# Turning attention probabilities on VectorE and by DMA through HBM in place of TensorE transposes

## What is computed

```python
def chunked_rel_attention(q, k, v, rel_bias):      # 8 heads of 64, 512 positions
    ...
    scores = jnp.einsum("bnqhd,bnkhd->bnhqk", qc, kb) * (dh ** -0.5)
    ...
    scores = jnp.where(valid, scores + bias[None, None], NEG_INF)
    p = jax.nn.softmax(scores, axis=-1)
    out = jnp.einsum("bnhqk,bnkhd->bnqhd", p, vb)

def hybrid_layer(x, norm_gain, w_in, w_out, rel_bias, cos, sin):
    ...
    y = jnp.concatenate([ya * jax.nn.silu(ag.astype(jnp.float32)),
                         yr * jax.nn.silu(rg.astype(jnp.float32))], axis=-1).astype(x.dtype)
    return x + y @ w_out.astype(x.dtype)
```

## Time and profile before

| | us |
|---|---|
| median of 3 runs | 1205.54 (1205.5 to 1205.58) |
| the profiled execution | 1205.41 |
| its span, first to last instruction | 1203.6 |
| PE busy in it | 1195.3 |
| DVE busy | 804.2 |
| ACT busy | 552.8 |
| POOL busy | 374.4 |

### The profile page before, as it was taken

One profiled execution on the slowest core, in us unless ns is written; L12 is line 12 of the kernel. 1 busy time (PEld: TensorE's weight loads), 2 busy tenths in 40 slices (PEclk: granted clock), 3 DMA queues, 4 the chain that ended last, 5 costly groups with the idle time before them and its releaser, 6 DMA issues.

```text
span 1203.6 us, 15005 instructions
## 1 busy us (share of the span) xinstructions
PE 1195.3 (99%) x5822; PEld 1007.5 (84%) x5822; DVE 804.2 (67%) x1402; ACT 552.8 (46%) x954; POOL 374.4 (31%) x275
## 2 busy tenths in 40 slices
PE   9999999999999999999999999999999999999998
PEld 7888888888888888888888889898888889898886
DVE  5878735466888536663568776666866866667875
ACT  6567532324444314332434465654334556654433
POOL 0135289997000000000000227765303023465200
PEclk9999999999999999999999999999999999999999
DMA  8233332323323322333223343433223334442251
GB/s 303 75 126 136 108 112 88 105 77 99 105 88 107 103 88 88 105 105 98 78 83 109 116 137 140 137 132 99 79 70 89 120 129 139 135 138 83 88 146 71
DMA packets 47000, 133.42 MB, mean 111 GB/s; under 512 B 4944, under 2 KB 11600, under 8 KB 46928
## 3 DMA queue, kind: packets, MB, share of 16 engines
q1 hardware_dynamic: 46496, 132.01, 33.7%
q10 hardware_dynamic: 432, 0.44, 0.1%
HBM read 114.08 MB, written 2.10 MB: 97 GB/s over the span
## 4 chain that ended last, share of the span: by engine, by line
PE 95%; DVE 2%; DMA 1%; POOL 1%; ACT 1%; issue 0%; ACTq 0%
PE ps L297 93%; PE ps L249 2%; DVE RA L274 1%; POOL FA L290 1%; DMA RA<-FA 0%; PE ps L551 0%; PE ps L492 0%; DVE FA L286 0%; ACT RA L266 0%; DVE FA L813 0%; DMA FA<-pvec 0%; DVE FA L274 0%; ACT FA L271 0%; ACT FA L270 0%; ACT RA L270 0%
## 5 line engine op out<-in xcount | busy, mean ns | idle before, releaser
L297 PE MATMUL ps<-RA 128*128 128x512 f32 (+1 forms) x5470 | 1176.7, 375 | 1.8 <-POOL RA L555 1.3
L297 PEld LDWEIGHTS ps<-RA 128*128 128x128 f32 x5470 | 974.0, 188 | 182.2 <-POOL RA L555 1.3
L274 DVE TENSOR_TENSOR RA<-FA,RA 128x1024 fp32r<-128x1024 f32 (+6 forms) x303 | 322.9, 1077 | 173.2 <-ACT RA L266 171.4
L266 ACT ACTIVATE RA<-FA 128x1024 fp32r<-128x1024 f32 (+5 forms) x338 | 280.7, 855 | 343.6 <-PE ps L297 177.6
L290 POOL TENSOR_SCALAR FA<-FA 128x256 f32<-128x256 f32 (+3 forms) x117 | 143.3, 1237 | 163.9 <-DVE FA L294 162.8
L286 DVE SCALAR_TENSOR_TENSOR FA<-ps,FA 128x512 f32<-128x512 f32 (+4 forms) x161 | 102.1, 638 | 90.7 <-PE ps L297 44.5
L274 POOL TENSOR_TENSOR FA<-FA 128x512 f32<-128x512 f32 (+1 forms) x82 | 108.9, 1330 | 87.0 <-ACT FA L270 66.7
L274 POOL TENSOR_TENSOR RA<-FA,RA 128x512 fp32r<-128x512 f32 (+1 forms) x37 | 69.6, 1890 | 109.6 <-ACT RA L266 109.6
L1233 POOL MEMSET FA<- 64x64 f32 x2 | 0.2, 144 | 328.7 <-ACT RA L266 328.7
L271 ACT ACTIVATE FA<-FA 128x512 f32<-128x512 f32 (+4 forms) x108 | 59.6, 552 | 80.4 <-DVE FA L1419 66.4
L270 ACT ACTIVATE FA<-ps,FA 128x512 f32<-128x512 f32 x56 | 38.1, 684 | 108.3 <-PE ps L297 108.3
(11 more groups left out here) (49 smaller groups left out, 278.4 us busy)
## 6 DMA issues: line engine op xcount, KB each, us to landing
FA<-w_units SPq DMA_DIRECT2D x188, 512.0 KB, 3.5
UA<-FA SPq DMA_DIRECT2D x32, 320.0 KB, 2.5
RA<-FA SPq DMA_DIRECT2D x10, 512.0 KB, 3.2
FA<-w_units SPq DMA_DIRECT2D x8, 384.0 KB, 3.0
FA<-x SPq DMA_DIRECT2D x8, 256.0 KB, 6.0
FA<-x_rows SPq DMA_DIRECT2D x4, 512.0 KB, 9.2
FA<-rel SPq DMA_DIRECT2D x16, 128.0 KB, 3.3
FA<-dmat SPq DMA_DIRECT2D x8, 256.0 KB, 2.8
```

The source lines that it names most:

```text
L266: return lambda eng: eng.activation(dst, src, ACT.Copy)
L274: return lambda eng: eng.tensor_tensor(dst, a, b, op)
L297: return lambda e: e.matmul(dst, a, b, start=start, stop=stop_)
```

## The change

The probabilities of block 2's attention heads are no longer scaled and no longer turned on PE. In `half_soft` a new `half_store` has DVE turn 128x640 as 32x32 squares into a staging buffer (`vt`); SP then stores it in four DMAs (one for each block of 32 partitions, in runs of 640 bytes) to a tensor in HBM, so that the squares land in their turned places. `half_load`, one slot later, loads the 128x640 back into `TPF` in rows of 2560 bytes. `half_split` reads that instead of PSUM, two slots after the scores as before. The values stay three slots after.

The reciprocals of the sums are taken once for a head, turned by DVE (`rt`), stored to HBM as a row (`rs`) and loaded as a broadcast over 64 partitions (`rl`, `spread_rows`); POOL multiplies the gated output by them, in one more instruction for each pair of heads.

Other edits: in `pieces_after`, `m` and `e` are queued ahead of the `pl`; seven weight low parts of each layer go from POOL to DVE (`POOL_LOW` keeps `g5` and `g6`), and so does the low part of the retention heads' q; in layer 0, `z` waits for the `vt` of its slot; the accumulator `ACC` is freed by `yl` and no longer by `yg`.

```diff
-POOL_LOW = {f"{l}{u}" for l in range(2) for u in ("q0", "v7", "k5", "q6", "q7", "k7", "g5", "g6", "g7")}
+POOL_LOW = {f"{l}{u}" for l in range(2) for u in ("g5", "g6")}
...
-                G(f"z.{k}", [f"f1q.{k}", f"0x.f{k}"], ts(hk, hk, F(PV + PV_GF + k, 1), ALU.mult))
+                G(f"z.{k}", [f"f1q.{k}", f"0x.f{k}", f"0vt.{(k + 2) // 2}.{k % 2}"], ts(hk, hk, F(PV + PV_GF + k, 1), ALU.mult))
...
-                (G if w == "q" else V)(f"{key}.l", [f"{key}.h"], sub(R(lo), F(t), Rf(h)))
+                V(f"{key}.l", [f"{key}.h"], sub(R(lo), F(t), Rf(h)))
...
-                    for i in pair:
-                        V(f"{pre}r.{h}.{i}", [f"{pre}e.{h}.{i}"], recip(F(RD2 + i, 1), F(DE + i, 1)))
-                    for i in pair:
-                        w = 128 * (i + 1)
-                        pc = PB + hoff[i]
-                        G(f"{pre}pn.{h}.{i}", [f"{pre}r.{h}.{i}"], ts(F(pc, w), F(pc, w), F(RD2 + i, 1), ALU.mult))
-                    dma(f"{pre}pm.{h}.{half}", [f"{pre}pn.{h}.{i}" for i in pair] + take(f"tp{half}"),
-                        U(TP + 640 * half, 640).bitcast(F32), F(PB + 640 * half, 640), f"pm{half}")
-                    for i in pair:
-                        free(f"pb{i}", f"{pre}pm.{h}.{half}")
+                    half_store(h, half)
...
-            def half_turn(h, half):
-                for n, i in enumerate(((3, 0), (2, 1))[half]):
-                    ...
-                    for j in range(i + 1):
-                        after = [f"{pre}pm.{h}.{half}"] + take(f"bank{b}") if j == 0 else []
-                        T(f"{pre}pT.{h}.{i}" if j == i else None, after,
-                          turn(bank(b, 128, 128 * j), U(TP + hoff[i] + 128 * j, 128)))
+            def half_store(h, half):
+                pair = ((3, 0), (2, 1))[half]
+                V(f"{pre}vt.{h}.{half}", [f"{pre}e.{h}.{i}" for i in pair] + take("vt"), lambda e: e.transpose(
+                    steps(F(VT, 1), [[32, 5], [160, 4], [1, 32]]), F(PB + 640 * half, 640).rearrange(
+                        "p (t c j) -> p t c j", t=5, c=4)))
+                for i in pair:
+                    free(f"pb{i}", f"{pre}vt.{h}.{half}")
+                for a in range(4):
+                    dma(f"{pre}st.{h}.{half}" if a == 3 else f"{pre}st.{h}.{half}.{a}",
+                        [f"{pre}vt.{h}.{half}"] + (take(f"turned{half}") if a == 0 else []),
+                        bass.AP(turned[half].tensor, turned[half].offset + 160 * a, [[640, 32], [20480, 4], [1, 160]]),
+                        steps(F(VT, 1, 32 * a, 32 * a + 32), [[160, 4], [1, 160]]), f"st{half}")
+                free("vt", f"{pre}st.{h}.{half}")
+                if half == 1:
+                    V(f"{pre}r.{h}", [f"{pre}e.{h}.{i}" for i in range(4)] + ["fill.2"], recip(
+                        steps(F(RDC, 1), [[8, 4], [1, 1]]), F(DE, 4).rearrange("p (i o) -> p i o", o=1)))
+                    V(f"{pre}rt.{h}", [f"{pre}r.{h}"] + take("rdt"), lambda e: e.transpose(F(RDT, 32), F(RDC, 32)))
+            def half_load(h, half):
+                dma(f"{pre}ld.{h}.{half}", [f"{pre}st.{h}.{half}"] + take(f"tp{half}"),
+                    TPF[0:128, 640 * half:640 * half + 640], turned[half], f"ld{half}")
+                ...
+                    dma(f"{pre}rs.{h}", [f"{pre}rt.{h}"] + take(f"rows{h % 2}"),
+                        rows[h % 2].rearrange("(n j) -> n j", j=32), FA[0:128:8, RDT:RDT + 32], "rs")
+            def spread_rows(h):
+                ...
+                dma(f"{pre}rl.{h}", [f"{pre}rs.{h}", "gemm.0q0"] + (take("db") if h % 2 == 0 else []), Rf(DB, 512, p, p + 64),
+                    rows[h % 2].rearrange("(o n) -> o n", o=1).to_broadcast([64, 512]), "rl")
...
-                for c in fins + splits + fins + splits + soft:
-                    next(c, 0)
+                for h, half in loads:
+                    half_load(h, half)
+                for c in fins:
+                    next(c, 0)
+                for c in splits:
+                    next(c, 0)
+                for c in fins:
+                    next(c, 0)
+                for c in soft:
+                    next(c, 0)
+                for c in splits:
+                    next(c, 0)
```

More of the change, by code:

```diff
@@ L51 @@
 PR = Z + 26368
+DB = Z + 29952
 R_COLS = Z + 30720
-TP, TI = 0, 1280
+TI = 0
 T_COLS = TI + 128
@@ L230, in two_blocks_kernel @@
         UA = ctx.enter_context(nc.sbuf_tensor("UA", [128, T_COLS], F32R))
+        TPF = ctx.enter_context(nc.sbuf_tensor("TPF", [128, 1280], F32))
+        turned = [nc.dram_tensor(f"turned{i}", (128, 640), F32, kind="Internal").ap() for i in range(2)]
+        rows = [nc.dram_tensor(f"rows{i}", (512,), F32, kind="Internal").ap() for i in range(2)]
         PS = [ctx.enter_context(nc.psum_tensor(f"ps{i}", [128, 512], F32)) for i in range(8)]
@@ L1224, in two_blocks_kernel @@
             return finish()
-        NM, DE, RD2 = columns(4), columns(4), columns(4)
+        NM, DE, RDC, RDT = columns(4), columns(4), VT + 640, VT + 672
         SS2, MS2, RC2, R12, TMP2 = columns(4), columns(4), columns(4), columns(4), columns(4)
@@ L1233, in two_blocks_kernel @@
             G(f"fill.{i}", ["acl.21", "sin"], lambda e, i=i: e.memset(F(HK + 512 * i, 64, 0, 64), MASKED))
+        G("fill.2", ["sin"], lambda e: e.memset(F(RDC, 32), 1.0))
         zero("z2", K2P, 2048, ["gemm.br7"])
@@ new lines, in half_load @@
+            def half_load(h, half):
+                dma(f"{pre}ld.{h}.{half}", [f"{pre}st.{h}.{half}"] + take(f"tp{half}"),
+                    TPF[0:128, 640 * half:640 * half + 640], turned[half], f"ld{half}")
+                free(f"turned{half}", f"{pre}ld.{h}.{half}")
+                if half == 1:
+                    dma(f"{pre}rs.{h}", [f"{pre}rt.{h}"] + take(f"rows{h % 2}"),
+                        rows[h % 2].rearrange("(n j) -> n j", j=32), FA[0:128:8, RDT:RDT + 32], "rs")
+                    free("rdt", f"{pre}rs.{h}")
@@ L1456, in half_split @@
+            def spread_rows(h):
+                p = 64 * (h % 2)
+                dma(f"{pre}rl.{h}", [f"{pre}rs.{h}", "gemm.0q0"] + (take("db") if h % 2 == 0 else []), Rf(DB, 512, p, p + 64),
+                    rows[h % 2].rearrange("(o n) -> o n", o=1).to_broadcast([64, 512]), "rl")
+                free(f"rows{h % 2}", f"{pre}rl.{h}")
             def half_split(h, half):
@@ L1460, in half_split @@
                     if h < 8:
[L1461 to L1464, removed]
+                        tile = (hoff[i] - 640 * half) // 128
+                        src = steps(TPF[0:128, 640 * half + 32 * tile:640 * half + 32 * tile + 1],
+                                    [[32, i + 1], [160, 4], [1, 32]])
+                        d = lambda c, i=i: steps(R(c + 128 * i, 128), [[384, i + 1], [32, 4], [1, 32]])
+                        parts.append((i, src, d(P2H), d(P2L), f"{pre}ld.{h}.{half}", None))
                     else:
@@ L1472, in half_split @@
                     V(f"{pre}pl.{h}.{i}", [f"{pre}ph.{h}.{i}"], sub(dl, src, dh.bitcast(F32)))
-                    free(where, f"{pre}pl.{h}.{i}")
+                    if where:
+                        free(where, f"{pre}pl.{h}.{i}")
+                if h < 8:
+                    free(f"tp{half}", *[f"{pre}pl.{h}.{i}" for i in ((3, 0), (2, 1))[half]])
             def head_values(h):
@@ L1499, in head_finish @@
                         p = h // 2
[L1500 to L1504, removed]
+                        G(f"{pre}ym.{p}", [f"{pre}yr.{h}", f"{pre}yr.{h - 1}", f"{pre}gt.{p}"],
+                          mul(F(ACC), F(ACC), F(SG + 512 * (p % 2))))
+                        free(f"sg{p % 2}", f"{pre}ym.{p}")
+                        G(f"{pre}yg.{p}", [f"{pre}ym.{p}", f"{pre}rl.{h}", f"{pre}rl.{h - 1}"], mul(
+                            F(ACC).rearrange("p (i a j) -> p i a j", i=4, a=4), F(ACC).rearrange("p (i a j) -> p i a j", i=4, a=4),
+                            steps(Rf(DB, 1), [[32, 4], [128, 4], [1, 32]])))
+                        free("db", f"{pre}yg.{p}")
                         def split():
-                            A(f"{pre}yh.{p}", [f"{pre}yg.{p}"], copy(R(YAH + 512 * p), F(t)))
-                            G(f"{pre}yl.{p}", [f"{pre}yh.{p}"], sub(R(YAL + 512 * p), F(t), Rf(YAH + 512 * p)))
-                            free(tn, f"{pre}yl.{p}")
+                            A(f"{pre}yh.{p}", [f"{pre}yg.{p}"], copy(R(YAH + 512 * p), F(ACC)))
+                            G(f"{pre}yl.{p}", [f"{pre}yh.{p}"], sub(R(YAL + 512 * p), F(ACC), Rf(YAH + 512 * p)))
+                            free("acc", f"{pre}yl.{p}")
                         later.append(split)
@@ L1561, in pieces_after @@
                 turns = lag(2, False) + lag(1, True)
+                loads = lag(1, False)
                 news = scores_at.get(s, [])
@@ L1564, in pieces_after @@
                     head_values(h)
-                for h, half in turns:
-                    half_turn(h, half)
+                    if h < 8:
+                        spread_rows(h)
```

8 lines of the change are left out of this document (2 added, 6 removed).

## The result

| | before | after |
|---|---|---|
| median, us | 1205.56 (1205.5 to 1205.6) | 1192.88 (1192.41 to 1194.84) |
| ratio, with its 95% interval | | 0.9898 [0.9881, 0.9915] |
| the profiled execution, us | 1205.41 | 1192.73 |
| its span, us | 1203.6 | 1190.9 |

The kernel is 12.7 us faster. On another chip, beside the last three experiments, it took 1193.06 us (1192.99 to 1194.43) against 1205.77, a ratio of 0.9898 [0.9884, 0.9913]. The lines of the program have moved: 302 is now every matmul, 279 a two-input operation, 271 an ACT copy, 295 a scaling, 208 a DMA from SP, 1445 the `vt`, 1425 the maxima; where an experiment adds a line, the numbers behind it are one higher.

The account below looks back on a forecast made before the run. PE (TensorE), busy 1195.3 of 1203.6 us, was taken to bound the kernel. 1205.5 - 12.8 (transposes removed) + 1.0 (waits from POOL contention in layer 0) = 1193.7 us, range 1191.8 to 1203.0.

Parts of the forecast that it names:

- The way the kernel is bound: Whole run: PE is busy 1195.3 of 1203.6 us, so each microsecond of PE work removed is worth a microsecond.
- 32 groups, 12.8 us: Block 2: 32 groups of five PE transposes, alternating 0.38 and 0.42 us, go; 12.8 us is the whole possible gain.
- `vt`, 0.85 us: VectorE's 32x32 transpose of 128x640 per half was estimated at 0.85 us, between 0.61 and 1.23.
- Price on the path: nothing: Slot 9: `vt` falls into time where VectorE sat idle or did reciprocals that go, so it costs PE nothing.
- Stores and load: Way through HBM: stores land in 2.3 to 3.2 us, load issued at once, 2 to 3 us room before the high part.
- Order on VectorE: Maxima ahead of `pl`: room before the values of 1.9 to 0.9 us in slot 9, 1.1 to 0.2 in slot 11.
- z and x1 in layer 0, 1.0 us: POOL's z and x1, now later, delay wl; PE waits at values of heads 0 to 3, 0 to 2.0 us, taken 1.0.
- The moved low parts, 0, bounds 0 to +1 a layer: 14 weight low parts and retention heads' q low parts go from POOL to VectorE: 0, bounds 0 and +1 us a layer.
- The sum: Whole kernel: 1205.5 - 12.8 + 1.0 = 1193.7 us.
- Rival 1: PE waits for `pl` at most heads, 0.3 to 0.6 us for each of 16: 1197.5 to 1202.3 us; chance 0.17.
- Rival 2: Staging buffer sets the beat: `vt` waits for stores, binding from a 3.9 us landing; 1215 us at 4.6; chance 0.13.
- rival 3: No change: either of the other two rivals stops near break-even, 1203 to 1208 us; chance 0.06.

Follow-up runs that it names:

- the last three experiments: Each against the changed kernel: `vt` done twice, 1201.69 us; `z` not waiting for `vt`, 1195.01 us; load issued ahead of the row of sums, 1193.22 us.
- The removal alone: The kernel before without its 160 PE transposes and nothing in their place, so probabilities stay unturned: 1193.19 us, ratio 0.9896.

## Why the prediction was right, step by step

- **The way the kernel is bound.** Right: PE stayed at 99%, and the time fell by what left PE. The forecast of 1193.7 lies 0.8 us above the median. But two terms missed, and they cancel in part.
- **32 groups, 12.8 us.** Too small. I lined up the matmuls of the two traces one by one, leaving out the 160: across the attention of the two layers the changed kernel gains 6.8 and 7.3 us, 14.1 in all, 0.44 us a group. The earlier trace rows show only 0.38 and 0.42 for the five transposes; a whole beat there, 0.38 + 7.35 + 0.42 + 6.21, is 14.36 us, and the same two slots now take 13.47 (from the values at 765.14 to those at 778.61), 0.89 less. So the matmuls between also got 0.09 us shorter, why is not shown: the whole beat was the number to take, not the transposes in it. The removal alone gains 14.5 by the same count, and loses 1.7 again where PE enters the retention heads.
- **`vt`, 0.85 us.** Right: 0.844. By the figure of the page "VectorE: DVE Perf Modes" of the Trainium skill (The three transpose paths) I had estimated 1.6; the measurement decides. Its advice (Rules for kernel authors) to leave such a transpose to TensorE didn't hold here, where TensorE bounds the kernel.
- **"Price on the path: nothing".** Right for one, and with less to spare than I wrote: a second one costs 8.6 us.
- **Stores and load.** Stores landed in 2.1 us, below my 2.3 to 3.2. The load took 4.1, above 3.2: here I was wrong. It is issued right behind a weight unit, or a unit and a row; in the kernel where it goes out behind its stores it took 2.9, while the stores, now behind the weight unit, took 3.5. "Issued at once" was wrong too: for every second half SP came to the load only 1.0 us (the median) after the stores had landed. In the slot that I laid out, counted from the end of `vt`, the stores had landed after 3.2 us (forecast 4.2 to 4.8), the load went out at 5.0 and landed at 10.4 (forecast 6.9 to 8.0). So the 2 to 3 us of room before the high part weren't there: its start lay under 0.1 us behind the landing in 14 of 32 halves and over 2 us in only two. ScalarE's 11 waits are the result. What took them up is the room behind the high part, which I had named without a number.
- **Order on VectorE.** I gave rooms of 1.9 to 0.9 and 1.1 to 0.2 us. They came out at 0.07 to 1.57 in layer 0 and 0.90 to 2.02 in layer 1, 0.18 at the place of the earlier trace rows. Right on the whole, with two of 16 below my smallest. What I didn't see is that the order is needed: the old one costs 18.5 us, first of all at the maxima.
- **z and x1 in layer 0, 1.0 us.** Wrong in place: PE waited at no values of heads 0 to 3. The room of head 4, 0.18, went to another POOL instruction beside wl, the multiplication by the sums, which I had put down at nothing; at head 5, with 0.07, no POOL instruction ran, and wl had waited for ScalarE's high part.
- **The moved low parts, 0, bounds 0 to +1 a layer.** Inside the bounds: PE is 0.5 us late once in each layer, at the first retention head's low parts.

```profile
831.95 1.29 POOL L279 TENSOR_TENSOR FA<-FA 128x512 f32<-128x512 f32 x1 [0.96 <-DVE FA L279]
832.70 1.92 DVE L279 TENSOR_TENSOR RA<-FA,RA 128x384 fp32r<-128x384 f32 x3
...
834.13 2.10 PE L302 MATMUL ps<-RA 128*128 128x512 f32 x12 [0.26 <-DVE RA L279]
```

  But "0" was the balance of a gain and a loss. With the low parts on POOL the change gains 7.5 us less, and with one more addition on VectorE 3.7 us less.
- **The sum.** -14.1 + 1.0 at these two places + 0.4 in the first microseconds of the run, where all matmuls started that much later, is -12.7. Mine was -12.8 + 1.0. That a 1.0 stands in both is luck: mine was meant for the values of layer 0, the measured one is PE's lateness at the retention heads, which I had put at 0.
- **The rivals.** Rival 1 didn't come: `pl` was in time at all heads, at two by 0.18 us or less. Rival 2 didn't come, since stores landed in 2.1 us; it came, with 3.5, when SP issued them late and behind a weight unit. Its chance of 0.13 was not too high. The place of the load alone would have been enough for it: 1209 us, a little beyond rival 3's break-even.

## What to carry to other kernels

Where one engine is busy for 99% of the time, take work off it even at a poor price elsewhere, and price the removal by the period of the whole beat, not by the removed instructions. Then look for what the other engines' queues have left: here an instruction of 0.84 us on VectorE, a load issued one slot sooner, or the maxima behind the low parts cost 8.6, 16 and 18.5 us, as much as the change brings or nearly so. A round trip through HBM can be hidden if nobody stands in a queue for it, and that hangs on the place of its issues among the others.

## What the runs showed of the hardware

- A VectorE transpose of 128x640 float32 in 32x32 squares, with a strided output, takes 0.844 us; one of 128x32 takes 0.21.
- The same transfer landed sooner or later with its place in SP's queue: 2.1 or 3.5 us for the stores, 4.1 or 2.9 for the load, the slower one each time in the kernel where a 512 KB weight unit is issued just ahead. Inside the second kernel the same: stores issued right behind a weight unit landed in 3.9 us (median of 13 halves), those issued some 2 us behind it in 2.0 (of 7), and those with a row in between in 3.1 to 3.8. That the weight unit is the cause is the likeliest reading; it was not taken away by itself.
- A row of 2 KB, broadcast to 128 KB, takes 4.6 us to land, longer than 320 KB of the load.
- PE's granted clock was 0.53 in the stretch after a wait of 1.66 us and 1.00 after one of 1.59 us in the same kernel, and 0.50 after one of 2.74 us in another. What told them apart is open. Where PE waited at most heads, 54.6 us of lateness at waits brought 23.1 us more in matmuls at the lower clock.
